# Compressed branch, first units and mixer residual: seven edits to a decoder layer on one core

## The reference

```
h = rms_norm(x, pre_mix_g); mem_n = rms_norm(mem, mem_norm_g)
o_nsa = g0 * compressed(q, k_c, v_c) + g1 * selected(q, k_s, v_s) + g2 * window(q, k_w, v_w)
compress(t) = gelu((blocks of 32 positions, stride 16, of t + pos) @ w1) @ w2
merged = sum_i sigmoid(gate_i) * (branch_i @ w_i)        # nsa, moba, memory
x = x + rms_norm(merged @ w_mix_out, post_mix_g)
h = rms_norm(x, pre_ffn_g)
x = x + rms_norm((silu(h @ w_gate) * (h @ w_up)) @ w_down, post_ffn_g)
```

## Time and profile before

| | us |
|---|---|
| median of 3 executions | 435.16 |
| lowest and highest | 435.12, 436.64 |
| the profiled execution's own time | 435.16 |
| its span (first to last instruction) | 433.4 |
| PE busy | 415.7 (96%) |
| DVE busy | 272.0 (63%) |
| ACT busy | 241.7 (56%) |
| POOL busy | 57.4 (13%) |

### The profile page before, as it was taken

The page is one execution under the profiler, slowest core; times in us unless marked ns, Lnnn a source line. Parts: engine busy times, 40 slices in busy tenths (PEclk is TensorE's granted clock), DMA queues, the critical chain, the costliest instruction groups (busy, mean ns, idle before and its releaser), DMA issues.

```text
span 433.4 us, 5858 instructions
## 1 busy us (share of the span) xinstructions
PE 415.7 (96%) x2044; PEld 338.6 (78%) x2044; DVE 272.0 (63%) x464; ACT 241.7 (56%) x410; POOL 57.4 (13%) x88
## 2 busy tenths in 40 slices
PE   5999979999999999999999899999999999999994
PEld 3788869977878877878787688888888888888883
DVE  4864994787666768638966666555555555545434
ACT  5654856568676776744365595445544554535321
POOL 5020540012211211217003300000000000000000
PEclk9999999999999999999999999999999999999999
DMA  8999973335533443357563738555556666555102
GB/s 292 393 335 365 370 227 133 103 102 190 159 134 99 148 144 97 100 193 265 171 195 101 229 110 281 169 172 168 182 190 194 194 194 188 170 174 195 49 2 97
DMA packets 51840, 78.80 MB, mean 182 GB/s; under 512 B 2044, under 2 KB 28424, under 8 KB 51816
## 3 DMA queue, kind: packets, MB, share of 16 engines
q1 hardware_dynamic: 50200, 73.79, 51.8%
q0 software_dynamic: 1328, 4.43, 3.2%
q10 hardware_dynamic: 288, 0.28, 0.2%
HBM read 77.42 MB, written 1.07 MB: 181 GB/s over the span
## 4 chain that ended last, share of the span: by engine, by line
PE 86%; DVE 7%; issue 3%; ACT 2%; DMA 1%; POOL 1%; POOLq 0%; DVEq 0%; ACTq 0%
PE acc L1148 25%; PE acc L1147 25%; PE acc L1146 25%; PE ob L1363 3%; DVE wl L769 2%; PE ptb L1331 2%; PE ob L1264 2%; PE sbank L1280 1%; PE ptb L1443 1%; PE sbank L1281 1%; ACT wh L488 1%; DMA gx<-in_gx 1%; PE sbank L1250 1%; DVE gates L982 1%; POOL yb L462 1%
## 5 line engine op out<-in xcount | busy, mean ns | idle before, releaser
L769 DVE TENSOR_TENSOR wl<-raw,wh 128x1024 fp32r<-128x1024 f32 (+1 forms) x129 | 158.2, 1234 | 92.7 <-ACT wh L488 92.5
L488 ACT ACTIVATE wh<-raw 128x1024 fp32r<-128x1024 f32 (+1 forms) x129 | 133.8, 1045 | 93.9 <-PE acc L1148 86.6
L1146 PE MATMUL acc<-wh,xh 128*128 128x512 f32 (+1 forms) x380 | 149.4, 393 | 0.3 <-DVE xl L803 0.2
L1148 PE MATMUL acc<-wh,xl 128*128 128x512 f32 (+1 forms) x380 | 149.0, 392 | 0.0
L1147 PE MATMUL acc<-wl,xh 128*128 128x512 f32 (+1 forms) x380 | 148.6, 391 | 0.0
L1146 PEld LDWEIGHTS acc<-wh,xh 128*128 128x128 f32 x380 | 72.5, 191 | 16.1 <-issue 1.9
L1148 PEld LDWEIGHTS acc<-wh,xl 128*128 128x128 f32 x380 | 71.4, 188 | 14.9
L1147 PEld LDWEIGHTS acc<-wl,xh 128*128 128x128 f32 x380 | 71.6, 188 | 13.8
L1146 PE MATMUL acc<-wh,ah 128*128 128x512 f32 x88 | 34.3, 390 | 0.0
L1148 PE MATMUL acc<-wh,al 128*128 128x512 f32 x88 | 34.3, 389 | 0.0
L1147 PE MATMUL acc<-wl,ah 128*128 128x512 f32 x88 | 34.2, 389 | 0.0
(11 more groups left out here) (192 smaller groups left out, 439.3 us busy)
## 6 DMA issues: line engine op xcount, KB each, us to landing
raw<-in_w_in SPq DMA_DIRECT2D x19, 1024.0 KB
raw<-in_w_ffn_gate SPq DMA_DIRECT2D x22, 512.0 KB
raw<-in_w_ffn_up SPq DMA_DIRECT2D x22, 512.0 KB
raw<-in_w_ffn_down SPq DMA_DIRECT2D x22, 512.0 KB
raw<-in_w_mix_out SPq DMA_DIRECT2D x4, 1024.0 KB
raw<-in_w_mem_kv SPq DMA_DIRECT2D x2, 1024.0 KB
raw<-in_w_nsa_o SPq DMA_DIRECT2D x2, 1024.0 KB
tb<-g_scratch SPq DMA_DIRECT2D x1, 1536.0 KB, 17.1
```

The costliest lines, as they stand in the source:

```text
L488: nc.scalar.activation(wh[:, k, :, 0:w], raw[:, slot, 2 * half:2 * half + 2, 0:w], ACT.Copy).then_inc(hi_done, 1)
L769: nc.vector.tensor_tensor(wl[:, k, :, 0:w], raw[:, slot, 2 * half:2 * half + 2, 0:w], wh[:, k, :, 0:w].bitcast(F32), ALU.subtract).then_in ...
L1146: nc.tensor.matmul(bank[:, 0:w], h[:, k, c], wh[:, slot, s, 0:w], start=first, stop=False)
L1148: return nc.tensor.matmul(bank[:, 0:w], l[:, k, c], wh[:, slot, s, 0:w], start=False, stop=last)
```

## The change

1. **Warm-up.** PE starts with three float32 matmuls of `eps` by itself into `ptb` (512, 512 and 256 columns), which wait for `eps` alone. DVE's memset of `ptb` is gone.
2. **Pieces.** All of block 0 is cut in 8 pieces of one row block (`first_hi(k)`, `first_lo(k)`, `first_block`), with x columns and weights loaded alternately for pieces 4 and 5, and 6 and 7; ACT issues the x columns 2 and 3. Counts of `hi_done`, `lo_done` move accordingly.
3. **Compressed branch's input.** It is batch 0 now and is turned into two banks (`sbank[0]` and `ptb`) behind step 8; ACT spreads keys (4 instructions) and DVE values (4 instructions) straight out of PSUM to `gcmp`. `kvc`, its copy and POOL's 8 instructions are gone. Both batches of queries move one step later.
4. **32nd column.** `gcmp` has 32 columns instead of 30: column 30 is zero, column 31 holds the position terms, put there by POOL at the start; their product with `w1` is computed once and added later.
5. **Column groups.** `compress_1` swaps operands: `gcmp` (32 columns) is loaded, `w1` (128 columns) moves, and four successive j go to four groups of 32 output partitions. All 32 matmuls stand behind step 18. DVE copies the 128 x 256 result to `sums`, and two matmuls by a constant (`add_column_groups`) behind step 19 add the four groups and the position row.
6. **Mixer's residual.** DVE does all four halves (`add_residual`); POOL's `residual` is gone. In tile 1 the order of rounding, gain and residual is changed on ACT and DVE, and `new_x_bank(1, n)` stand behind different steps on PE.
7. **Addresses.** `G_ROOM`, `small` and a spacer keep tiles behind the larger constants at the same address remainders.

The core of the diff:

```diff
-                nc.vector.tensor_copy(kvc[:], bank).then_inc(qk_ev[0], 1)
+                    for g in range(GROUPS):
+                        for jj in range(2):
+                            ins = nc.vector.tensor_copy(gcmp[HD * jj:HD * jj + HD, 1, :, NCMP * g:NCMP * g + NCMP],
+                                                        bass.AP(src.tensor, src.offset,
+                                                                [src.ap[0], [2, PAIRS], [CMP_STRIDE, NCMP]]))
...
+            for k in range(PIECES):
+                x_hi(k)
+                first_hi(k)
+            split[0] = SUBS
...
+            def first_block(after):
+                for k in range(PIECES):
+                    slot, s = k // 2, k % 2
+                    pe.wait_ge(hi_done, k + 1)
+                    for t in range(TILES):
+                        nc.tensor.matmul(acc[:, 0, t], xh[:, k, P * t:P * t + P], wh[:, slot, s], start=(k == 0), stop=False)
+                    pe.wait_ge(xl_done, k + 1)
+                    pe.wait_ge(lo_done, k + 1)
+                    for t in range(TILES):
+                        nc.tensor.matmul(acc[:, 0, t], xh[:, k, P * t:P * t + P], wl[:, slot, s], start=False, stop=False)
+                        ins = nc.tensor.matmul(acc[:, 0, t], xl[:, k, P * t:P * t + P], wh[:, slot, s], start=False,
+                                               stop=(k == PIECES - 1))
...
-                for kv, j in steps[11 * part:11 * part + 11]:
-                    ins = nc.tensor.matmul(ob[:, 2 * NCMP * kv:2 * NCMP * (kv + 1)], w1[:, kv, j, :], gcmp[:, kv, j, :],
-                                           start=(j == 0), stop=(j == PAIRS - 1))
+                for kv in range(2):
+                    for j in range(PAIRS):
+                        c = 32 * (j % 4)
+                        ins = nc.tensor.matmul(ob[c:c + 32, CMP_HID * kv:CMP_HID * (kv + 1)], gcmp[:, kv, j, :], w1[:, kv, j, :],
+                                               start=(j < 4), stop=(j >= PAIRS - 4))
...
+            def add_column_groups():
+                pe.wait_ge(cmp_dve, 1)
+                for kv in range(2):
+                    ins = nc.tensor.matmul(ob[:, 256 + 2 * NCMP * kv:256 + 2 * NCMP * (kv + 1)], sums[:, kv], add_groups,
+                                           start=True, stop=True)
...
+            still = bass.AP(eps, 0, [[1, P], [0, 512]])
+            pe.wait_ge(eps_set, 1)
+            for w in (512, 512, 256):
+                nc.tensor.matmul(ptb[:, 0:w], still[:, 0:P], still[:, 0:w], start=True, stop=True)
...
-                               1: [lambda: qk_batch(5, 4, [col(C_KM), col(C_KM + P)]), lambda: compress_1(0)],
-                               2: [lambda: compress_1(1)],
-                               3: [lambda: compress_1(2)]})
+                               1: [lambda: qk_batch(5, 4, [col(C_KM), col(C_KM + P)])],
+                               2: [compress_1],
+                               3: [add_column_groups]})
```

More of the change, by code:

```diff
@@ L327, in _ @@
                 sp.dma_start(raw[:, 0, s], w_in[:, s, 0:SLICE]).then_inc(sub0d[s], 16)
-            sp.dma_start(gx[:, x_columns(2, 4)], gxt[:, x_columns(2, 4)]).then_inc(xtd[2], 16)
             sp.dma_start(raw[:, 0, 2:4], w_in[:, 2:4, 0:SLICE]).then_inc(loaded[0], 32)
-            sp.dma_start(gx[:, x_columns(4, 8)], gxt[:, x_columns(4, 8)]).then_inc(xtd[3], 16)
-            plain(1, w_in, 4, 0)
+            for half in range(2):
+                k = 4 + 2 * half
+                sp.dma_start(gx[:, x_columns(k, k + 2)], gxt[:, x_columns(k, k + 2)]).then_inc(xtd[3 + half], 16)
+                load = sp.dma_start(raw[:, 1, 2 * half:2 * half + 2], w_in[:, k:k + 2, 0:SLICE])
+                if half == 0:
+                    load.then_inc(sub2d, 16)
+                else:
+                    load.then_inc(loaded[1], 32)
             plain(2, w_in, 0, SLICE)
@@ L413, in _ @@
             nc.gpsimd.dma_start(w2v[:], a["cmp_w2_v"][0]).then_inc(cmpd, 16)
[L414 to L428, removed]
+            pool.wait_ge(qk_pe, QK_COMPRESS + 1)
             nc.gpsimd.memset(vcz, 0.0).then_inc(zeroed, 1)
@@ L1137, in _ @@
                 gain(1, 1, t, B_DOWN)
-                finish(1, t, 6 + t, 5, fin_done)
+                norm(t, 6 + t, 5, 8)
+                for n in range(2):
+                    add_residual(1, t, n, 5, fin_done)
         @block.tensor
@@ L1166, in free_acc, with whole_block @@
                     pe.wait_ge(ev[t], b - 1)
-            def whole_block(b, v0, subs, h, l, k0=0, w=SLICE, ready=None, after=None, first=0):
+            def whole_block(b, v0, subs, h, l, k0=0, w=SLICE, ready=None, after=None):
                 free_acc(b)
-                for i in range(first, subs):
+                for i in range(subs):
                     if ready is not None:
@@ L1491 @@
     sees_block = (rows >= CMP_LEN - 1).astype(np.float32)
-    arrays["in_const0"] = np.concatenate([eye, sees_block], axis=1)
+    group_rows = np.eye(CMP_W, GROUPS * NCMP, dtype=np.float32)
+    group_rows[CMP_POS] = 1.0
+    arrays["in_const0"] = np.concatenate([eye, sees_block, np.tile(group_rows, (P // CMP_W, 1))], axis=1)
     arrays["in_onehot"] = bucket_onehot()
```

245 lines of the change are left out of this document (127 added, 118 removed).

## The result

The changed kernel takes 424.64 us (median of 4 runs, 424.40 to 426.55), beside 435.9 for the kernel before on the same chip (4 runs, 435.12 to 436.74): a ratio of 0.9747, 95% interval 0.9726 to 0.9768. The kernel before runs in two clusters: of 18 runs later on, 11 took 434.8 to 435.5 us at a mean granted clock of 0.997 to 0.999, and 7 took 436.6 to 437.0 at 0.994 or 0.995.

A forecast was written before the change was run, and what follows sets the result against it. PE is busy 415.7 of 433.4 us, but up to 60.6 us DVE's stream, started by a queued transfer, sets the clock. 435.16 - 5.2 (to batch 6) - 1.3 (mixer) = 428.7 us; 0.90 lies from 426.0 to 432.2.

The forecast's parts named there:

- The start: Warm-up and pieces end block 0 at 18.0 us, 2.3 us earlier on PE; none reaches the sum, unit 6 being queue-pinned.
- DVE's stretch: DVE from 41.05 us to block 3's evacuation: -1.7 us; PE still waits about 2 us at batch 4, until 58.9.
- The relief from POOL: DVE's steps without POOL's 8 instructions: -2.6 us, from four `meml` steps 1.8, the next weight step 0.5, later four 0.3.
- compress_1: Compressed branch's 64 matmul records on PE: four column groups at once, 2.3 us instead of 6.9; bounds 1.7 and 6.9.
- (a): Rival at the column groups: PE's queue, not the array, paces them; 4.3 us, total 430.2 us; chance 0.15.
- (b): Rival at the column groups: they run one after another; 6.9 us, total 432.6 us; chance 0.05.
- (f): Rival at the column groups: records in one bank wait for each other's ends; +7.9 us, total 443; chance 0.04.
- -5.2: Total gain in us by batch 6, forecast at 78.5 instead of 83.67, from DVE's stretch and the compressed branch.
- The mixer: Residual moved from POOL to DVE at the mixer's end: -1.3 us, with four DVE waits of 0.3 to 0.7 us.
- the bound of -2.5: Upper limit of the mixer's gain, in us: all of PE's waits there gone; the other bound was 0.
- Addresses: Addresses, the 32nd column and constants: 30 extra columns in a 65 KB load, hidden; 0 us.
- Rival (c): Rival at the start: the queue doesn't pin unit 6 and the start's 2.3 us come through; 426.4 us; chance 0.10.

## Why the prediction was wrong

Point by point, by its own steps:

- **The start: right.** The fast pace came at 6.55 us (forecast about 7), block 0 ended at 17.99 (18.0), unit 6 stayed pinned (39.64 beside 39.96), and taking the whole edit out changes the time by 0.2 us. The step had the gain end up in the stall at batch 4, as it did alone (2.37 to 3.69 us), but did not ask what a longer stall does to the clock.
- **DVE's stretch: mechanism right, size off.** I took -1.7 and it was -2.2 within the stretch, and 0.3 more came from unit 6. The relief from POOL was 3.2 us where I took 2.6: the first four `meml` steps gave 1.9 (1.8), the weight step behind them 0.5 (0.5), the later four 0.5 (0.3), and the last two weight steps 0.3 (none). Those two had run beside POOL's copy to `tbc`. They do so in the changed kernel too, and there the copy took longer (2.8 us in place of 1.9) and they did not. PE's wait at batch 4 was 1.1 us, not about 2: PE was there at 57.05, as forecast, and DVE was done at 58.05, not 58.9.
- **compress_1: right in kind, 0.4 us too dear.** 1.9 us on the path, 2.3 forecast and near the lower bound of 1.7; rivals (a), (b) and (f) fall. With the last point that makes batch 6 at 77.26, not 78.5: -6.4 in place of **-5.2**.
- **The mixer: right.** -1.6 in the trace, with a little pace in it, and -1.4 to -1.5 alone; -1.3 forecast. Two waits for DVE, 0.67 and 0.47 us, not four. (The waits of the earlier trace rows make 2.3 us, so the bound of -2.5 was 0.2 too wide.)
- **Addresses: the step that failed.** "Addresses, the 32nd column and the constants: [...] hidden; 0" counted only the load's bytes. Moving `xl` from remainder 0 to 128 was worth 2.8 us. The sentence "from 104 to 230 us PE is busy for 125.16 of 126 us" was read as a stretch in which nothing changes; it should have said that any change of pace shows there in full. The rows for a doubt were there: in the kernel before, matmuls on `ah` and `al`, which stand as `wh` and `wl` do, had means of 389 to 391 ns between 360 and 415 us, and the matmul on `xl` 397. That the tiles' remainders must agree was in no row; the experiments show it, while why PE is slower when they differ stays open.

The sum by what was measured: 435.16 - 6.4 - 1.6 - 2.8 = 424.4. Two thirds of the miss of 4.3 us are the missing term. The parts alone add up to 5.6 + 1.5 + 2.9 + 0.2 = 10.2 us. The remaining 0.6 probably arises only together: batch 4 stands at 59.25 with the compressed branch's edit alone and at 58.44 with all but the start. No run separates it from the scatter of single runs, which is of the same size. Rival (c) named 426.4, the nearest of all, but for a mechanism that did not act.

## What to carry to other kernels

A change of buffer sizes is a change of addresses, and belongs into the sum when an engine is saturated: compare the mean duration of one matmul form across tensors that stand differently, and multiply by all of them. An edit that only shortens work ahead of a pinned wait is worth nothing: it lengthens the stall, and in the three profiles here with a stall of 2.71 us or more between stretches of work the clock fell.

## What the runs showed of the hardware

- Matmuls of 512 columns went faster when the tile that PE loads and the one that it streams had the same remainder of 256 bytes in their start addresses. With `wh` and `wl` at 128, `xl` at 128 is fast and at 0 and 64 slow (some 11 ns per group of three, in which one matmul has unlike tiles); with them at 0, `xl` at 0 is fast and `ah`, `al` at 128 slow (395 ns in place of 389, on each of the three); all at 0 is fast. That 256 is the right period was not tried.
- Transfers into SBUF went at 395 to 406 GB/s with the destinations at remainder 0, beside 342 to 354 with them at 128. Over 20 to 40 us together the 13 kernels with all at 128 had 344 to 349, the two with all at 0 had 401 and 400, and the one with `raw` and the first x at 0, but memt0, mems and x0 at 128, had 364.
- 64 matmul records that load 32 columns took 0.030 us each with a new column group at each step and 0.067 with eight in a row to one group.
- DVE's `meml` steps took 0.82 or 0.83 us beside POOL's additions in one kernel and 0.94 or 0.95 in the kernel before, and four without POOL 1.67 together.
- The granted clock fell to 0.50 (1.2 GHz) at stalls of PE of 2.71, 3.46 and 3.69 us in the profiles, with PE at work before and after: 1.1 us after PE went on in the first, 0.8 us before it in the second, 0.5 us after it in the third. It did not fall at stalls of 2.47, 2.37 and 1.10 us. It was low for 3.4 us in the first and the last, which cost 1.6 us each (compress_1 starts at 65.98 and 65.91 us, in the kernel before at 64.32), and for 6.8 us in the second, which cost 2.8 and is the slowest of its runs (429.06). The kernel before with its two clusters fits this: its profile, at 435.16, has no such fall, and of its 41 runs beside the experiments those above 436.3 have a mean granted clock of 0.993 to 0.995, the others 0.997 to 0.999. At which instruction the clock fell in those runs was not traced, so that it is this stall is an inference.
